# Products that nobody reads, put into two waits of TensorE in the first layer's mixer

## What is computed

```
h = rms_norm(x, g_mix); proj = h @ w_in          # c_q, c_kv, k_rope, and 1792 features
# attention group, 8 heads, blocks of 128 queries
q, k, v = ...                                     # from c_q and c_kv, normed, rotated
scores = einsum('bqhd,bkhd->bhqk', q, k) * scale, masked
probs = softmax(scores); out = einsum('bhqk,bkhd->bqhd', probs, v)
# recurrent group, 8 heads of 64
w = -softplus(-(w0 + tanh(wl) @ w2)) - 0.5        # "low rank w"
a = sigmoid(a0 + al @ a2)                         # "low rank a"
kk = k * k_k;  kk = kk * rsqrt(sum(kk * kk) + 1e-12)   # key norms, per head
```

## Time and profile before

| | us |
|---|---|
| median of 3 runs | 1866.36 (1866.13 to 1868.05) |
| profiled execution, its own time | 1868.89 |
| its span | 1867.1 |
| PE busy | 1734.4 (93%) |
| DVE busy | 444.2 (24%) |
| ACT busy | 198.7 (11%) |

### The profile page before, as it was taken

The page is one execution under the profiler, slowest core; times in us unless marked ns, Lnnn a source line. Parts: engine busy times, 40 slices in busy tenths (PEclk is TensorE's granted clock), DMA queues, the critical chain, the costliest instruction groups (busy, mean ns, idle before and its releaser), DMA issues.

```text
span 1867.1 us, 21630 instructions
## 1 busy us (share of the span) xinstructions
PE 1734.4 (93%) x9470; PEld 926.4 (50%) x9470; DVE 444.2 (24%) x767; ACT 198.7 (11%) x334; POOL 42.2 (2%) x126
## 2 busy tenths in 40 slices
PE   7888987767899999999999999999999999999898
PEld 5678764434764444548554333344343334444443
DVE  2666532111642000037341010101101011010003
ACT  1342021111121000010210000000000000000001
POOL 5002000000000000000000000000000000000000
PEclk9978999888999999999999999999999999999999
DMA  7022369999864432362647999999999999999990
GB/s 275 3 108 75 127 249 422 422 422 415 330 233 174 149 135 67 121 251 65 231 181 301 411 415 411 416 397 411 416 410 416 410 416 398 410 413 414 413 384 26
DMA packets 136507, 548.22 MB, mean 294 GB/s; under 512 B 7585, under 2 KB 12818, under 8 KB 109282
## 3 DMA queue, kind: packets, MB, share of 16 engines
q1 hardware_dynamic: 133280, 540.67, 73.4%
q0 software_dynamic: 1664, 5.05, 0.8%
q10 hardware_dynamic: 1474, 1.19, 0.3%
HBM read 543.51 MB, written 1.05 MB: 292 GB/s over the span
## 4 chain that ended last, share of the span: by engine, by line
PE 69%; DMA 22%; DVE 5%; ACT 2%; SPq 1%; issue 1%; DVEq 0%; ACTq 0%
DMA ring<-in_exp_w 15%; PE ps L2036 13%; PE ps L2043 8%; DMA ring<-in_w_down 7%; PE ps L1744 4%; PE ps L2076 4%; PE ps L1919 4%; PE ps L1893 4%; PE ps L1934 4%; PE ps L1791 3%; PE ps L2084 3%; PE ps L1683 2%; PE ps L1455 2%; PE ps L1863 1%; PE ps L1831 1%; PE ps L1574 1%
## 5 line engine op out<-in xcount | busy, mean ns | idle before, releaser
L2036 PE MATMUL ps<-ring,xT 128*128 128x512 f32 x672 | 293.0, 594 | 7.7 <-DMA ring<-in_exp_w 6.9
L2043 PE MATMUL ps<-ring,xT 128*64 128x512 f32 (+3 forms) x1536 | 224.5, 480 | 8.9 <-DMA ring<-in_exp_w 8.9
L2036 PEld LDWEIGHTS ps<-ring,xT 128*128 128x128 f32 x672 | 126.8, 190 | 168.8 <-issue 156.9
L2076 PE MATMUL ps<-ring,work 128*128 128x512 f32 x336 | 151.6, 610 | 11.7 <-DMA ring<-in_exp_w 10.1
L2043 PEld LDWEIGHTS ps<-ring,xT 128*64 128x64 f32 (+1 forms) x1536 | 86.8, 128 | 138.0 <-issue 110.0
L2968 DVE TENSOR_TENSOR work<-work,ps 128x512 f32<-128x512 f32 (+3 forms) x32 | 38.5, 1204 | 467.7 <-PE ps L2036 342.5
L2084 PE MATMUL ps<-ring,work 128*64 128x512 f32 (+1 forms) x672 | 111.6, 524 | 1.7 <-DVE work L2978 1.6
L2076 PEld LDWEIGHTS ps<-ring,work 128*128 128x128 f32 x336 | 64.8, 195 | 95.1 <-issue 93.2
L1203 ACT ACTIVATE work<-ps 128x512 f32<-128x512 f32 (+3 forms) x32 | 21.1, 661 | 732.5 <-PE ps L2036 407.5
L1661 PE MATMUL ps<-ring,work 128*32 128x256 f32 x976 | 64.9, 414 | 21.5 <-DMA ring<-in_w_up 20.4
L1744 PE MATMUL ps<-xT,ring 128*128 128x256 f32 x384 | 83.4, 380 | 0.0
(11 more groups left out here) (523 smaller groups left out, 1562.5 us busy)
## 6 DMA issues: line engine op xcount, KB each, us to landing
ring<-in_exp_w SPq DMA_DIRECT2D x168, 2048.0 KB, 23.4
ring<-in_w_up SPq DMA_DIRECT2D x32, 1024.0 KB, 18.6
ring<-in_w_down SPq DMA_DIRECT2D x32, 1024.0 KB, 18.5
ring<-in_dense_w SPq DMA_DIRECT2D x15, 2048.0 KB, 8.0
ring<-in_w_gate SPq DMA_DIRECT2D x29, 1024.0 KB, 18.0
ring<-in_w_in SPq DMA_DIRECT2D x6, 2048.0 KB, 14.2
ring<-in_w_in SPq DMA_DIRECT2D x8, 1104.0 KB, 15.4
ring<-in_w_out SPq DMA_DIRECT2D x4, 2048.0 KB, 12.1
```

Source lines behind the costliest of these rows:

```text
L2036: ins = mm(ps[:, bank + b, :], slots_k(m, k), w[:, i, b * 512:(b + 1) * 512], start=start, stop=stop)
L2043: ins = mm(ps[n * j:n * (j + 1), bank, 0:c], slots_k(m, k), columns, start=start, stop=stop, tile_position=(0, n * j))
L2076: ins = mm(ps[:, 4 + b, :], turned[:, 4 * a + c, :], w[:, c, b * 512:(b + 1) * 512], start=(first and c == 0), stop=(final and c == 3))
```

## The change

`keep_warm` is defined earlier in PE's list, with the same body, and is called twice more: eight products into bank 0 between the turnings of q and k and the wait for "kk rec", and nine products into bank 3 between `features(5)` and the wait for "probs 1". Bank 0 was last read by "qk read 1" and is written next by `low_rank(0, "w")`; bank 3 was last read by "sig a" and is written next after "pT 0". Nothing else is changed.

```diff
+            def keep_warm(n, bank):
+
+                for _ in range(n):
+                    mm(ps[:, bank, 0:2 * P], before[:, :], x_sb[:, 0, 0:2 * P], start=True, stop=True)
+
             def qkv(t):
...
             pe.wait_ge(*dve_f("qk 1"))
             turn_qk(1)
+            keep_warm(8, 0)
             pe.wait_ge(*dve_f("kk rec"))
             pe.wait_ge(*act_f("raw 4"))
...
             pe.wait_ge(*act_f("sig a"))
             features(5)
+            keep_warm(9, 3)
 
             pe.wait_ge(*act_f("probs 1"))
...
-            def keep_warm(n, bank):
-
-                for _ in range(n):
-                    mm(ps[:, bank, 0:2 * P], before[:, :], x_sb[:, 0, 0:2 * P], start=True, stop=True)
-
             def places(stage, n):
```

## The result

| | before | after |
|---|---|---|
| median, us | 1867.19 (8 runs, 1865.44 to 1868.62) | 1872.34 (8 runs, 1865.02 to 1873.23) |
| ratio | | 1.0021, 95% interval 1.0011 to 1.0031 |
| profiled execution, its own time | 1868.89 | 1872.54 |
| its span | 1867.1 | 1870.8 |

The change makes the kernel slower by 0.2%, where I had forecast 3 us less. The three first runs of before had a median of 1866.36, all eight 1867.19. One of the eight runs after took 1865.02; the other seven lie between 1871.5 and 1873.2.

A forecast was written before the change was run, and what follows sets the result against it. Bound: the first quarter's chain through PE, DVE and ACT, where waits let PE's clock fall. First wait -3.0, second 0, behind -0.1: -3.1 us off 1866.4 gives 1863.3 us, range 1857.0 to 1867.5.

The forecast's parts named there:

- Part 1, overshoot: Wait for the reciprocal: idle products end at 95.20, 0.9 us late, but the clock does not fall at 95.6.
- Part 1, the scores: L1370 at full clock takes 3.46 us; the scan then limits, so the scores' masking starts 3.0 us earlier, at 103.9.
- rival D: Clock falls at about 95.6 despite the first wait's idle products; masking 1.5 us later, total 1867.9 us; chance 0.11.
- Part 2, cost: Wait for the exponentials: idle products end at 117.1, 0.7 us before probs 1 is due; cost 0.
- Part 2, gain: Products with v (L1395, L1399): clock falls again, gain 0; bound 5.2 us if they run at full clock.
- Rival B: Clock also holds through the second pair of waits, products with v at full clock: 3.0 + 5.2 = 8.2, 1858.2 us; chance 0.28.
- Behind it, the clock: After the products with v: shift moves work against later clock changes, between -3 and +1 us, taken as -0.1.
- Behind it, the supply: Issue gap of 2.61 us at 142.97 amid L1415: added instructions can move it, +2.6 or -2.6 us, taken as 0.
- Rival E: rival D plus a second issue gap brought on by the added instructions: 1.5 + 2.6 = 4.1 us, 1870.5 us; chance 0.05.
- Passing on: First layer's expert weights: DMA starts again 3 us earlier, so the front's saving passes to the end.

The follow-up runs named there:

- Run 9: Kernel before plus only the first wait's eight idle products, six before the reciprocal and two before the scores, padded to 256 instructions: 1861.12 us, ratio 0.9969.
- 4: The change without keep_warm(8, 0), so only the nine products before the exponentials, no padding: 1867.86 us, ratio 0.9995 to before.
- 7: Kernel before plus only the nine idle products before the exponentials, padded to 256 instructions: 1861.91 us, ratio 0.9970.
- 8: As 7, with two more idle products in each of the two short waits behind, 13 in all, padded to 256 instructions: 1862.42 us, ratio 0.9966.
- 10: Kernel before plus the split first wait of Run 9 and the 13 products of 8, padded to 256 instructions: 1858.40 us, ratio 0.9952.
- 2: The changed kernel with 47 tiny products at the start of PE's list, 256 added instructions in all: 1864.44 us, ratio 0.9989 to before.
- 6: Kernel before plus only the eight idle products before the reciprocal, in one piece, padded to 256 instructions: 1866.04 us, ratio 0.9987.
- run 1: Kernel before with 17 tiny products at the start of PE's list, 68 added instructions, nothing in the two waits: 1872.33 us, ratio 1.0022.

## Why the prediction was wrong, point by point

**Part 1, overshoot.** L1361 was to start at 95.20; it started at 95.10. The low rank products were to end at 98.85; L1376 starts at 98.98. The clock was to hold past 95.6 and up to 99; it held to 98.8. Right.

**Part 1, the scores.** L1370 at 3.46 us was wrong: 7.01. Here the forecast took it that a clock once held stays, though the means of 0.59 over the 12.55 us and of 0.54 over 104 to 106 in the earlier trace rows showed PE at work on just these products from 95.6 to 105.8 at half clock. The sentence behind rival D, that a fall in L1370 would cost "at most 0.3", was wrong by its own numbers: 16 records at half clock take 6.9 us, 98.9 + 6.9 = 105.8 is behind the scan's 103.9. So of the 3.0 us 0.8 were left. Run 9 shows the 3.0 and more (3.8) when the clock is held.

**Part 2, cost.** The idle products, forecast to end 0.7 us before the exponentials, ended 1 us after them, as L1376 was late, and L1402 still started 0.8 us earlier, all of the shift: cost 0, as the two short waits took it up. Right.

**Part 2, gain.** Put at 0 with a bound of 5.2. In the changed kernel's profile it is 0 (L1402 at half clock, 6.42), in those of 4, 7, 8 and 10 it is the bound (3.79). Rival B, at 0.28, named this and the effect, 3.0 + 5.2, yet B did not happen in the profile after: the idle products did push L1392 against L1396, with 0.20 us between, and the clock fell at 126.2 all the same. What tips it between kernels 2 and 7, which differ by the eight products of the first wait, is open. The fall does not come at the same place of the program each time; in the profile of 6, with nothing in the second wait, it came at 119.1 and was over at 125.9, just after the products with v began at 125.20.

**Behind it, the clock.** A new low stretch appeared at 211.5 in the output projection (eight records in 5.39 us), 1.7 us lost that were back by 250. Within the bounds of -3 and +1.

**Behind it, the supply.** This is the step that failed and turned the sign. I saw the issue gap at 142.97, wrote that added instructions can move it, and took 0. It moved and was 2.0 us shorter, within the bound of 2.6, and by 156 us nothing of that was left. I did not list PE's waits for "issue" over the whole run: they would have shown a second one, 2.77 us before L1601 at 479.05, behind a loop, with the DMA full, and the question would have been what stands behind it if the border moves by 68 instructions. Rival E had the mechanism (an issue gap brought on by the added instructions) at 0.05, tied to rival D, which was not what happened: it needs nothing of the front, as run 1 shows. And its price had a term missing: the gap itself cost 1.2, the half clock behind it 2.5, together 3.7, and E had only the gap, at 2.6.

**Passing on.** What the front gained passed the expert loop: 0.64 us at 256 and 0.34 at 474 in the change, and in 7 and 10 a lead of 5.1 and 10.4 us at 258 was still 5.0 and 10.4 at 490. Right. Behind 944 us each profile drifts by itself, with the clock at the routing of the second block: the lead of 10 is 10.4 at 945 and 7.5 at 959, and 4, 3.0 us ahead at 945, is 0.4 behind at 959. At the end 7 is 7.6 us ahead, 10 is 7.1.

## What to carry to other kernels

Instructions are not free where they cost no time: in a program with loops, count how many an edit adds to an engine's list and look at every wait for "issue" behind it. To judge an edit in the front, time it with its count filled up to 256, or beside a kernel that adds as many instructions that do nothing. And what idle products are worth goes by where they stand: with two of the eight placed ahead of the scores, where the products of the chain had let the clock fall, the gain was 0.31% in place of 0.13% (the difference, 0.18, has an interval of some 0.16 to either side).

## What the runs showed of the hardware that I had not expected

The supply of PE's instructions has borders that move with the count of added instructions and are back in place after 256. They were found to within one record in five kernels behind the loop (after 37, 38, 55, 53 and 8 records) and in all thirteen profiles amid L1415 (ahead of the last 7, 41, 40, 23, 25 and 70 records, and of the last 6 in all seven with 256 added). The gap at one was 1.4 to 3.3 us behind the loop, with the DMA at a share of 1.05, and 0.6 to 4.1 us amid L1415. Seventeen tiny products at the start of the list, in a wait of 10.96 us, made the kernel 0.22% slower at the other end.

PE at work with no pause on products that contract over 8, 64 and 96 rows (L1355, L1361, L1370) did not hold the clock: it was 0.50 from 95.6 to 105.8 before and from 98.8 to 105.7 after. It came back there with no product of 128 rows in between, while the last scores still ran. With two products of 128 rows ahead of the scores it did not fall (9 and 10). That the rows are what counts, and not something else in which the idle products differ, was not tested.

The same kernel's executions differ by more than one edit of this kind is worth: before lay between 1855.5 and 1872.4 in over 80 runs. A single profile shows the mechanism, not the size.
